# A two-block transformer in fp32r pieces: three buffers begin 9408 bytes later, and one product takes its matmuls in another order

## The chip, the cores and the metric

One core of a Trainium2 chip. The metric is the device time of one execution of the whole kernel in microseconds, the median of the runs.

## The reference

Two transformer-like blocks on one sequence of 256 tokens with 2048 features, all in float32. The first has causal differential attention and a gated linear recurrence side by side, attention to 256 memory rows, and a gated MLP with a causal convolution of three taps. The second has three convolution and pooling mixers and again such an MLP. Nearly all arithmetic is in 18 products with weight matrices. Those of the MLPs read

```
def conv_gated_mlp(h, w_up, conv_w, conv_b, w_down):
    up = h @ w_up                                      # 2048 -> 2 * 5632
    up = causal_depthwise_conv(up, conv_w) + conv_b
    gate, val = jnp.split(up, 2, axis=-1)
    return (jax.nn.silu(gate) * val) @ w_down          # 5632 -> 2048
```

## The kernel before

**Pieces of float32.** Each float32 operand is split in two fp32r pieces: a rounded part (hi) and its rest (lo). A product w x is computed as w_hi x_hi + w_hi x_lo + w_lo x_hi, summed in PSUM.

**Weights.** They come as 900 chunks of [128, 1024] (512 KB), one after another, through four slots. SyncE's queue loads a chunk into `raw`, ScalarE writes the rounded part into `w_hi` (line 784), VectorE the rest into `w_lo` (line 1325), TensorE multiplies and gives the slot back with the chunk's last matmul (`chunk_used`). A chunk holds 8 tiles of 128x128.

**Products, in the order of the run**, with their chunks: hg_fm 32, hg_i 16, da_fm 32, da_v 16, hg_g 16, mem_k 32, mem_v 32, out 32, mem_q 32, mem_o 32, up 176, down 88, conf 24, pool 8, gated 36, out_2 32, up_2 176, down_2 88. All plain matmuls go through the helper at line 2107. Four forms of order occur:

- Triples: for each tile w_hi with x_hi, w_hi with x_lo, w_lo with x_hi, 256 columns each, 24 matmuls in a chunk. Kind "F" and blocks without a kind in `product`: 148 chunks in hg_fm, mem_k, out, mem_q, mem_o, conf, pool and gated.
- Token-major in `product` (hg_i, da_v, mem_v: 64 chunks): the operand is stationary, the weights move, 512 columns, 12 matmuls in a chunk.
- Groups of four, two tiles in turn: a matmul of 512 columns takes the operand's hi and lo together with w_hi; it is done for two tiles, then w_lo with x_hi (256 columns) for the same two. 16 matmuls in a chunk. Kind "Q" in `product` (128 chunks in hg_fm, da_fm, hg_g, mem_k, out, mem_q, mem_o), and `TWO_TILES` in `product_halves` ("up" and up_2).
- Groups of four, `ROWS_TOGETHER` in `product_halves` ("down"): the same four matmuls, but for one tile and two rows k of the operand.

`product_tokens` (out_2, down_2) has tokens as output rows: per pair of slices hi with w_hi, hi with w_lo, lo with w_hi, 512 columns each, 12 in a chunk.

**The two orders of `product_halves`**, each a list of (kind, row, tile) for one chunk, are at lines 2209 and 2210. "up" and up_2 have 22 blocks of 8 chunks; a block fills four PSUM banks (one per tile), the next block the other four. VectorE and ScalarE read a block's banks once its last chunk is done; TensorE waits for that before it writes the same banks again two blocks later.

**Places.** `place` gives each buffer the next free bytes of the partition, from byte 16512 on. `raw`, `w_hi` and `w_lo` have 16384 bytes each; `x_res` (the residual x) has 16384 and `op` (the operand of most products, hi and lo of each of 16 slices side by side) 32768. Parameters, constants and small buffers follow with 9408 bytes together. Behind them begins the arena, at byte 124224, with everything else; `g` (the operand of "down" and down_2) and `y_hi` begin there. Some buffers are put on top of x and the operand by `x_at` and `op_at`.

Of the kernel before, what the change touches and what calls it, by code (L numbers as in the profile page):

```python
# [19 lines left out]
F32R = mybir.dt.float32r  # L20
# [5 lines left out]
P = 128  # L26
TOK = 256
DM = 2048
KT = DM // P
# [9 lines left out]
SLOTS = 4  # L39
CW = 1024  # L40
# [56 lines left out]
def plan():  # L97
    found, chunk, block = {}, 0, 0
    evac = {"act": 0, "dve": 0, "x": 0}
    for name, tiles, blocks, kt, token_major, reader in GEMMS:  # L100
        g = Gemm()
        g.name, g.tiles, g.blocks, g.kt, g.token_major, g.reader = name, tiles, blocks, kt, token_major, reader
        g.chunks = kt * tiles // 8
        g.first_chunk = chunk
        g.first_block = block
        g.banks = tiles // 2
        g.first_evac = evac[reader]
        g.before = found[GEMMS[len(found) - 1][0]] if found else None
        chunk += g.chunks * blocks
        block += blocks  # L110
        evac[reader] += g.banks * blocks
        g.end_chunk = chunk
        g.end_evac = evac[reader]
        found[name] = g
    return found, chunk
# [108 lines left out]
def build(nc, A):  # L224
    GM, NCHUNK = plan()
# [3 lines left out]
    with ctx:  # L229
        at = [16512]  # L230

        def place(name, shape, dt=F32, offset=None):
            size = 4
            for d in shape[1:]:
                size *= d
            where = at[0] if offset is None else offset
            if offset is None:
                at[0] += (size + 31) // 32 * 32
            return nc.alloc_sbuf_tensor_at(name, shape, dt, offset=where)
# [4 lines left out]

        raw = place("raw", [P, SLOTS, CW])
        w_hi = place("w_hi", [P, SLOTS, CW], F32R)
        w_lo = place("w_lo", [P, SLOTS, CW], F32R)
        x_at = at[0]
        x = place("x_res", [P, KT, TOK])
        op_at = at[0]  # L250
        op = place("op", [P, KT, 2, TOK], F32R)
        op_hi, op_lo = op[:, :, 0], op[:, :, 1]
        par = place("par", [P, NPAR])
        con = place("con", [P, NCON])
        small = place("small", [P, 64])
# [5 lines left out]
        tok_bias, tok_rstd = place("tok_bias", [P, 2]), place("tok_rstd", [P, 2])  # L261
        rstd = place("rstd", [P, 2, TOK])
        ones_r = place("ones_r", [P, P], F32R)
        arena = at[0]
        end = 229344
        room = end - arena
# [261 lines left out]
        def half_end(g, chunks):  # L528

            return [max(n for n, (of, _) in enumerate(chunks) if of == h) for h in range(4)]  # L530
# [784 lines left out]
        def _(dve):  # L1315
# [410 lines left out]
            def feed_forward(g, gd, turn, n, w, bname):  # L1726
# [6 lines left out]
                def gather(b, kind, parity):  # L1733
                    dve.wait_ge(first_kept, turn * g.blocks + 2 * b + kind + 1)
                    _, second = two_sums(parity, 0, 4)
                    TT(up[:, :, UPAD:UPAD + TOK], up[:, :, UPAD:UPAD + TOK], second, ALU.add).then_inc(dve_evac, 2)
# [368 lines left out]
        def _(pe):  # L2105
            def mm(out, lhsT, rhs, start, stop):
                return nc.tensor.matmul(out, lhsT, rhs, start=start, stop=stop, skip_group_check=True)  # L2107
# [101 lines left out]
            TWO_TILES = [(kind, r, 2 * u + t) for r in range(2) for u in range(2) for kind in (HI, LO) for t in range(2)]  # L2209
            ROWS_TOGETHER = [(kind, r, t) for t in range(4) for kind in (HI, LO) for r in range(2)]  # L2210

            def product_halves(g, both, ready, at=None, peeled=2, sequence=TWO_TILES):

                def one(b, parity):
                    static = isinstance(b, int)
                    if static:
                        past, pb_ = order[g.first_block + b - 2]
                        pe.wait_ge(evacs[past.reader], past.first_evac + past.banks * (pb_ + 1))  # L2220
                    else:
                        pe.wait_ge(evacs[g.reader], g.first_evac + g.banks * b - g.banks)
                    for c in range(g.chunks):
                        if at and static:
                            at(b, c)
                        s = (g.first_chunk + g.chunks * b + c) % SLOTS if static else c % SLOTS
                        pe.wait_ge(chunk_split, g.first_chunk + g.chunks * b + (c + 1))
                        if static and b == 0:
                            pe.wait_ge(operand_ready, ready(2 * c + 1))
                        for kind, row, t in sequence:  # L2230
                            k = 2 * c + row
                            cs = slice((4 * row + t) * P, (4 * row + t + 1) * P)
                            if kind == HI:
                                last = mm(ps[:, 4 * parity + t], w_hi[:, s, cs], both[:, k].rearrange("p a t -> p (a t)"), k == 0, False)
                            else:
                                last = mm(ps[:, 4 * parity + t, TOK:2 * TOK], w_lo[:, s, cs], both[:, k, 0], False, k == g.kt - 1)
                        last.then_inc(chunk_used, 1)

                for b in range(peeled):
                    one(b, (g.first_block + b) % 2)  # L2240
                pairs = (g.blocks - peeled) // 2
                if pairs:
                    with pe.Fori(0, pairs) as m:
                        for d in range(2):
                            one(2 * m + (peeled + d), (g.first_block + peeled + d) % 2)
# [28 lines left out]
            halves = lambda stage: (lambda k: READY[stage] + k // 2 + 1)  # L2274
# [264 lines left out]
            def beside_up(g, n):  # L2539

                def at(b, c):
                    if (b, c) == (1, 4):
                        pe.wait_ge(dve_evac, g.first_evac + g.banks)
                        sums(n)
                    if (b, c) == (2, 0):
                        pe.wait_ge(std_ready, STD_END[n])
                return at
# [86 lines left out]
            def turn_y(turn, j, t):  # L2634

                pe.wait_ge(y_scaled[t], 8 * turn + j + 1)
                for e in range(2):
                    f = 2 * j + e
                    bank = turn_banks(turn)[j]
                    last = nc.tensor.transpose(ps[:, bank, e * TOK + t * P:e * TOK + (t + 1) * P], y_tok[turn][:, t, f * P:(f + 1) * P], ident)  # L2640
                if t:
                    last.then_inc(y_turned, 1)
                elif j == 0:
                    last.then_inc(half_turned, 1)
# [32 lines left out]
            def beside_up_2():  # L2677
                sums_at = beside_up(GM["up_2"], 5)

                def at(b, c):  # L2680
                    if (b, c) == (0, 1):
                        turn_y(0, 2, 1)
                        turn_y(0, 3, 1)
                    for j in {1: (4, 5), 3: (6, 7)}.get(c, ()) if b == 0 else ():
                        pe.wait_ge(operand_ready, READY["up_2"] + j - 3)
                        turn_y(0, j, 0)
                        turn_y(0, j, 1)
                    sums_at(b, c)
                return at

            product_halves(GM["up_2"], op, halves("up_2"), beside_up_2(), 4, TWO_TILES)
            product_tokens(GM["down_2"], g_hi, g_lo, DOWN_2_CHUNKS, lambda pair: READY["down_2"] + 2 * pair + 2)
            for t in range(2):
                for q in range(4):
# [101 lines left out]
```

## Time and profile before

| | us |
|---|---|
| device time, median of 3 runs | 2654.44 |
| lowest, highest | 2654.02, 2654.53 |
| profiled execution: span, first to last instruction | 2652.2 |
| TensorE busy with matmuls | 2642.4 |
| VectorE busy | 1789.4 |
| ScalarE busy | 1345.5 |
| GpSimd busy | 150.3 |

The profiled execution has no device time of its own beside its span, so the span stands for it; the median of the runs is 2.2 us above it. Matmuls overlap: the next starts before the one before has ended, so their busy time says little, and the distance from start to start is what one costs. In the timeline, matmuls of one kind in a row are merged into one line with "x2", and the line's first number is the start of the first.

### The profile page before, as it was taken

How to read it: one execution, taken by the hardware profiler on the slowest of the kernel's cores; microseconds unless marked ns; L12 is line 12 of the kernel's file. 1: busy time of each engine (PE TensorE's matmuls, PEld its weight loads, DVE VectorE, ACT ScalarE, POOL GpSimd, SP SyncE). 2: the span in 40 equal slices, each digit the busy share in tenths (PEclk: the TensorE clock that was granted, in tenths of full speed). 3: DMA queues.
4: the chain of work that ended last, by engine and by line, in shares of the span. 5: the costliest groups of instructions: out<-in, count | busy, mean ns of one | idle time of the engine just before them, and what ended most of it. 6: DMA issues, size and time to landing. Idle time of an engine off the chain costs nothing.

```text
span 2652.2 us, 41690 instructions
## 1 busy us (share of the span) xinstructions
PE 2642.4 (100%) x15689; PEld 2332.9 (88%) x15689; DVE 1789.4 (67%) x2188; ACT 1345.5 (51%) x1647; POOL 150.3 (6%) x106
## 2 busy tenths in 40 slices
PE   9999999999999999999999999999999999999999
PEld 9888898889999888888888889998888888888887
DVE  7677567565645777777775456998777777776444
ACT  6554375464533655555553344444665555554443
POOL 2001200000200200000001222000020000000000
PEclk9999999999999999999999999999999999999999
DMA  8655456546545566566666665655566656656564
GB/s 260 192 160 187 139 182 185 178 154 203 177 129 167 184 192 189 188 188 188 188 189 191 190 190 173 196 187 174 168 191 190 190 189 187 187 188 206 191 192 148
DMA packets 256256, 487.12 MB, mean 184 GB/s; under 512 B 15069, under 2 KB 80629, under 8 KB 255616
## 3 DMA queue, kind: packets, MB, share of 16 engines
q1 hardware_dynamic: 254496, 476.11, 57.1%
q0 software_dynamic: 1488, 9.19, 1.0%
q8 instruction: 92, 1.51, 0.2%
q14 instruction: 36, 0.29, 0.0%
q10 hardware_dynamic: 144, 0.01, 0.0%
HBM read 483.12 MB, written 2.13 MB: 183 GB/s over the span
## 4 chain that ended last, share of the span: by engine, by line
PE 94%; DVE 4%; ACT 1%; POOL 1%; issue 0%; DVEq 0%; ACTq 0%; POOLq 0%
PE ps L2107 94%; DVE w_lo L1325 1%; DVE acc L1854 1%; POOL sumsq L724 1%; ACT w_hi L784 0%; DVE ya L1918 0%; DVE x_res L2088 0%; DVE ua L1359 0%; ACT lnz L1219 0%; PE ps L2640 0%; PE ps L2427 0%; DVE y_lo L1390 0%; DVE ya L1920 0%; DVE cvp L1908 0%; DVE ya L1914 0%
## 5 line engine op out<-in xcount | busy, mean ns | idle before, releaser
L1325 DVE TENSOR_TENSOR w_lo<-raw,w_hi 128x1024 fp32r<-128x1024 f32 x899 | 1119.2, 1247 | 785.6 <-ACT w_hi L784 784.4
L2107 PE MATMUL ps<-op,w_hi 128*128 128x512 f32 (+1 forms) x6208 | 1638.8, 353 | 0.1
L784 ACT ACTIVATE w_hi<-raw 128x1024 fp32r<-128x1024 f32 x899 | 949.4, 1059 | 1106.3 <-PE ps L2107 1088.2
L2107 PEld LDWEIGHTS ps<-op,w_lo 128*128 128x128 f32 x5024 | 948.4, 189 | 170.4
L2107 PE MATMUL ps<-op,w_lo 128*128 128x256 f32 x5024 | 1089.5, 279 | 0.0
L2107 PEld LDWEIGHTS ps<-op,w_hi 128*128 128x128 f32 x6208 | 955.2, 190 | 4.2 <-issue 1.8
L2107 PE MATMUL ps<-g,w_hi 128*128 128x512 f32 x704 | 219.6, 393 | 0.0
L2107 PE MATMUL ps<-w_hi,g 128*128 128x512 f32 x704 | 217.7, 390 | 0.0
L2107 PE MATMUL ps<-w_hi,op 128*128 128x512 f32 x512 | 163.5, 393 | 0.0
L2107 PEld LDWEIGHTS ps<-w_hi,g 128*128 128x128 f32 x704 | 132.1, 188 | 30.2
L2107 PEld LDWEIGHTS ps<-g,w_lo 128*128 128x128 f32 x704 | 132.4, 188 | 30.0
L2107 PE MATMUL ps<-g,w_lo 128*128 128x256 f32 x704 | 138.8, 279 | 0.0
L2107 PE MATMUL ps<-w_lo,g 128*128 128x512 f32 x352 | 138.7, 394 | 0.0
L2107 PEld LDWEIGHTS ps<-w_hi,op 128*128 128x128 f32 x512 | 96.1, 188 | 21.7 <-issue 1.3
L2107 PEld LDWEIGHTS ps<-g,w_hi 128*128 128x128 f32 x704 | 106.0, 188 | 0.0
L2107 PE MATMUL ps<-w_lo,op 128*128 128x512 f32 x256 | 99.8, 390 | 0.0
L2107 PEld LDWEIGHTS ps<-w_lo,g 128*128 128x128 f32 x352 | 66.2, 188 | 13.1
L1854 DVE SCALAR_TENSOR_TENSOR acc<-glu,par,acc 128x256 f32<-128x256 f32 x180 | 75.1, 478 | 0.0
L1751 DVE SCALAR_TENSOR_TENSOR cv<-up_s,par,cv 128x256 f32<-128x256 f32 x176 | 73.3, 478 | 0.0
L1751 DVE SCALAR_TENSOR_TENSOR cg<-up_s,par,cg 128x256 f32<-128x256 f32 x176 | 73.3, 478 | 0.0
L2107 PEld LDWEIGHTS ps<-w_lo,op 128*128 128x128 f32 x256 | 48.1, 188 | 9.3
L1740 DVE TENSOR_TENSOR up_s<-up_s,rstd 128x1024 f32<-128x1024 f32 x44 | 53.9, 1226 | 1.5
(318 smaller groups left out, 1534.6 us busy)
## 6 DMA issues: line engine op xcount, KB each, us to landing
raw<-in_weights SPq DMA_DIRECT2D x899, 512.0 KB, 4.5
x_res<-in_x SPq DMA_DIRECT2D x8, 256.0 KB, 5.6
mem_x<-in_mem POOLq DMA_DIRECT2D x1, 2048.0 KB, 8.8
x_res<-in_x POOLq DMA_DIRECT2D x1, 2048.0 KB, 9.9
w_row<-row_dram POOLq DMA_DIRECT2D x2, 1024.0 KB, 7.8
out_x<-x_res SPq DMA_DIRECT2D x3, 512.0 KB, 2.9
rel_rev<-rel_dram POOLq DMA_DIRECT2D x1, 1024.0 KB, 8.3
hg_con<-in_hg_consts POOLq DMA_DIRECT2D x1, 576.0 KB, 5.2
```

The costliest lines, as they stand in the source:

```text
L724: steps.inc(TT(sumsq[:, :, :], squares[:, 0] if j == 1 else sumsq[:, :, :], squares[:, j], ALU.add))
L784: nc.scalar.activation(w_hi[:, s], raw[:, s], ACT.Copy).then_inc(hi_rounded, 1)
L1325: TT(w_lo[:, s], raw[:, s], w_hi[:, s].bitcast(F32), ALU.subtract).then_inc(chunk_split, 1)
L1740: TT(up[:, :, UPAD:UPAD + TOK], up[:, :, UPAD:UPAD + TOK], spread(rstd[:, 1], 4), ALU.mult).then_inc(up_scaled, 1)
L1751: ins = STT(buf[:, t], up[:, t, tap:tap + TOK], col(tap, kind, t, b), buf[:, t], ALU.mult, ALU.add)
L1854: ins = STT(acc[:, i], glu[:, i, tap:tap + TOK], pc("conv_b_w_2", 6 * tap + i), acc[:, i], ALU.mult, ALU.add)
L2107: return nc.tensor.matmul(out, lhsT, rhs, start=start, stop=stop, skip_group_check=True)
```

## The change

The small buffers are placed ahead of `w_lo`, `x_res` and `op`, which so begin 9408 bytes later; the small buffers begin 65536 bytes earlier, and the arena stays where it was. In up_2 the order of a chunk's matmuls is `ROWS_TOGETHER` in place of `TWO_TILES`; "up" keeps `TWO_TILES`.

```diff
         raw = place("raw", [P, SLOTS, CW])
         w_hi = place("w_hi", [P, SLOTS, CW], F32R)
-        w_lo = place("w_lo", [P, SLOTS, CW], F32R)
-        x_at = at[0]
-        x = place("x_res", [P, KT, TOK])
-        op_at = at[0]
-        op = place("op", [P, KT, 2, TOK], F32R)
-        op_hi, op_lo = op[:, :, 0], op[:, :, 1]
         par = place("par", [P, NPAR])
         con = place("con", [P, NCON])
...
         rstd = place("rstd", [P, 2, TOK])
         ones_r = place("ones_r", [P, P], F32R)
+        w_lo = place("w_lo", [P, SLOTS, CW], F32R)
+        x_at = at[0]
+        x = place("x_res", [P, KT, TOK])
+        op_at = at[0]
+        op = place("op", [P, KT, 2, TOK], F32R)
+        op_hi, op_lo = op[:, :, 0], op[:, :, 1]
         arena = at[0]
...
-            product_halves(GM["up_2"], op, halves("up_2"), beside_up_2(), 4, TWO_TILES)
+            product_halves(GM["up_2"], op, halves("up_2"), beside_up_2(), 4, ROWS_TOGETHER)
```

The begin of a chunk of up_2 on TensorE, before the loop over its later blocks, the same in both kernels (`op` is the operand, `ps` the PSUM banks):

```order
L2107 MATMUL ps<-op,w_hi 128x512 [waits chunk_split]
L2107 MATMUL ps<-op,w_hi 128x512
L2107 MATMUL ps<-op,w_lo 128x256 x2
L2107 MATMUL ps<-op,w_hi 128x512 x2
L2107 MATMUL ps<-op,w_lo 128x256 x2
```

What moved isn't seen in such rows, since they name neither row nor tile. A group's first two matmuls were row 0 with tiles 0 and 1 and are now rows 0 and 1 with tile 0; the two with w_lo likewise. The first two wrote two banks and now write one.

## Rows read from the trace of the kernel before

**Rows 1.** The page: span, busy time and instructions by engine, granted clock, chain

```profile
span 2652.2 us, 41690 instructions
PE 2642.4 (100%) x15689; PEld 2332.9 (88%) x15689; DVE 1789.4 (67%) x2188; ACT 1345.5 (51%) x1647; POOL 150.3 (6%) x106
...
PEclk9999999999999999999999999999999999999999
...
PE 94%; DVE 4%; ACT 1%; POOL 1%; issue 0%; DVEq 0%; ACTq 0%; POOLq 0%
```

**Rows 2.** TensorE's waits, whole run: total us, times, longest us

```profile
PE ps L2107 <- DVE da_q L1412: 1.2, 1, 1.2
PE ps L2427 <- DVE attn L1654: 0.6, 1, 0.6
PE ps L2640 <- ACT y_tok L1244: 0.5, 1, 0.5
PE ps L2652 <- ACT y_tok L1244: 0.4, 1, 0.4
PE ps L2107 <- DVE w_lo L1325: 0.4, 2, 0.2
PE ps L2107 <- POOL sumsq L726: 0.4, 1, 0.4
```

**Rows 3.** The page's groups: busy us, mean ns, idle us before, releaser

```profile
L784 ACT ACTIVATE w_hi<-raw 128x1024 fp32r<-128x1024 f32 x899 | 949.4, 1059 | 1106.3 <-PE ps L2107 1088.2
```

**Rows 4.** TensorE in order of time, "up": start us, us, instruction

```profile
1000.02 0.63 PE L2107 MATMUL ps<-op,w_hi 128*128 128x512 f32 x2
...
1139.36 0.63 PE L2107 MATMUL ps<-op,w_hi 128*128 128x512 f32 x2
```

**Rows 5.** TensorE in order of time, up_2

```profile
2100.04 0.63 PE L2107 MATMUL ps<-op,w_hi 128*128 128x512 f32 x2
...
2239.37 0.63 PE L2107 MATMUL ps<-op,w_hi 128*128 128x512 f32 x2
```

**Rows 6.** TensorE in order of time, "down"

```profile
1400.45 0.39 PE L2107 MATMUL ps<-g,w_hi 128*128 128x512 f32 x1
...
1539.12 0.39 PE L2107 MATMUL ps<-g,w_hi 128*128 128x512 f32 x1
```

**Rows 7.** Busy us (x matmuls) by engine, clock, DMA share, GB/s: "up", up_2, "down"

```profile
1000.10:1139.30 139.20, 139.20 (x801) 121.44 (x800) 102.59 (x124) 75.82 (x86) 0.00 (x0) 1.00 0.60 188
2100.10:2239.35 139.25, 139.25 (x801) 121.48 (x801) 100.97 (x120) 77.53 (x90) 0.00 (x0) 1.00 0.61 188
1400.46:1539.10 138.64, 138.64 (x802) 121.62 (x801) 69.84 (x58) 53.03 (x51) 27.31 (x18) 1.00 0.62 190
```

**Rows 8.** TensorE in order of time, conf

```profile
1610.26 0.40 PE L2107 MATMUL ps<-op,w_hi 128*128 128x256 f32 x2
...
1610.62 0.40 PE L2107 MATMUL ps<-op,w_hi 128*128 128x256 f32 x2
```

**Rows 9.** TensorE in order of time, hg_i

```profile
129.95 0.84 PE L2107 MATMUL ps<-w_hi,op 128*128 128x512 f32 x3
...
131.31 0.84 PE L2107 MATMUL ps<-w_hi,op 128*128 128x512 f32 x3
```

**Rows 10.** TensorE in order of time, down_2

```profile
2499.64 0.62 PE L2107 MATMUL ps<-w_hi,g 128*128 128x512 f32 x2
...
2501.70 0.39 PE L2107 MATMUL ps<-w_hi,g 128*128 128x512 f32 x1
```

**Rows 11.** VectorE by line and shape, 900 to 1350 us ("up")

```profile
L1325 DVE TENSOR_TENSOR w_lo<-raw,w_hi 128x1024 fp32r<-128x1024 f32 x162 | 199.0, 1229 | 121.6 <-ACT w_hi L784 121.6
...
L1740 DVE TENSOR_TENSOR up_s<-up_s,rstd 128x1024 f32<-128x1024 f32 x20 | 24.5, 1226 | 0.7
```

## The prediction

> **What bounds the kernel now.** I read the page first, then who waited for whom on TensorE, then TensorE in order of time in one stage after another. [...] Busy time of pipelined matmuls proves little, so the waits have to confirm it: in the whole run TensorE's matmuls waited 3.5 us for anyone, in six lines [rows 2]. So the time is the sum of the distances from one matmul's start to the next one's. VectorE and ScalarE are ahead of it: most of ScalarE's idle time ends with TensorE giving back a slot of the weights [rows 3]. Only what changes TensorE's own pace, or makes another engine late by many microseconds, can be seen in the result.
>
> The pace is read from starts. A group of four matmuls (two of 512 columns with w_hi, two of 256 with w_lo) begins in "up" at 1000.02 us and, 200 groups later, at 1139.36: 139.34 / 200 = 696.7 ns [rows 4]. In up_2, which has the same order, it is 2239.37 - 2100.04 = 139.33, again 696.7 ns [rows 5]. In "down", which takes two rows of a tile together, it is 1539.12 - 1400.45 = 138.67, or 693.3 ns [rows 6]. (That 200 groups lie between is certain: one more or less would move the quotient by 3.5 ns per group, and the windows between count 800 or so matmuls with the one or two that lap over the edges [rows 7].) The granted clock is 1.00 in all three windows. The 3.3 ns are therefore no clock and no wait; something in the order or in the place of the operands costs them.
>
> What would be free of it? 1536 columns at 2.4 GHz take 640.0 ns, so "down" pays 53.3 ns above the columns, 13.3 per matmul. The products in triples pay the same: in conf three matmuls of 256 columns start every 0.36 us, 120 each, 13.3 above 106.7 [rows 8]; in hg_i six of 512 take 131.31 - 129.95 = 1.36 us, 226.7 each, 13.3 above 213.3 [rows 9]. So 13.3 ns is the floor that three different orders reach, and "up" and up_2 lie 3.3 ns per group above it. down_2 lies above it as well: nine matmuls in 2501.70 - 2499.64 = 2.06 us, 686.7 ns per three where hg_i has 680.0 [rows 10].
>
> **The change part by part.** Two edits; neither adds or removes an instruction, a transfer or a wait.
>
> *The order in up_2.* Its 22 blocks have 8 chunks each, 176 chunks of four groups. Each group keeps its four matmuls and their widths; only which row and tile they belong to changes. The nearest row is "down", with the same widths in the order that up_2 gets. At its pace a group saves 3.3 ns, a chunk 13.3 ns and the stage 176 x 13.3 = **2.35 us**, all of it on the path, since TensorE sets the pace there and nobody is made to wait longer: the weights' slot is given back by the last matmul of a chunk in either order, and the results are read only when a block's last chunk is done. But "down" differs from up_2 in a second thing, its moving operand g lies elsewhere. If the place and not the order gives "down" its pace, the edit gives nothing; and it could cost something, bounded by the largest excess that a row shows, 6.7 ns per three matmuls in down_2, taken once per group: 3.3 more than now, +2.35 us. I take the gain, because it is the row with the same widths and the same order, and keep -2.35 and +2.35 as ends.
>
> *The places.* From the shapes, w_hi begins at byte 32896, w_lo at 49280, the operand at 82048 and g at 124224. Modulo 128 these are 0, 0, 0 and 64. The shift of 9408 is 64 modulo 128, so w_lo and the operand move to 64, where g already is; w_hi stays. par, con and the other small buffers move down by exactly 65536 and keep all their low bits. Does the place cost anything? For VectorE the rows say no: a subtraction of 128x1024 with all its buffers at 0 takes 1229 ns in the middle of "up", a multiplication of up_s and rstd, both in the part that lies at 64, takes 1226 [rows 11]; I put nothing on VectorE, ScalarE and the transfers, and ScalarE's idle 1106.3 of 2652.2 us, nearly all behind TensorE, would cover some per cent more [rows 3]. For TensorE the large distances seem free: each window of 50 chunks goes twelve times round the four slots and six times through the operand's 16 rows, and two such windows agree to 0.01 us [rows 4, 5]. Only the low bits are open, since within one stage they never change. They could be worth anything from the best to the worst of the rivals below, -4.0 to +9.6 us over the other stages. I take 0, as the floor of 13.3 is reached both with moving operand and weights at 0 (hg_i, conf) and with g at 64 against weights at 0 ("down").
>
> *What is late next.* At the start of up_2 TensorE does wait, for 0.4 to 0.5 us at a time, for ScalarE and VectorE to hand over the turned rows [rows 2]. A chunk that is 13 ns shorter makes these waits 13 ns longer, so the first two or three chunks gain nothing: under 0.05 us, left out.
>
> Sum: the profiled span of 2652.2 becomes 2649.85. The times shown are device times, 2654.44 in the median (2654.02 to 2654.53), 2.2 us above the span, which I take to stay: **2652.1 us**, 0.09% less. A measurement of this kernel can tell about 0.2%, 5.3 us, from no change, so the forecast is "within 0.2%".
>
> **The rivals.**
>
> *Places at 64 give the pace of "down" to every two-tile order (faster).* Speaks for it: "down" is the only stage of such groups whose moving operand lies at 64, and the only one at the floor. Against: conf and hg_i reach the floor at 0. Besides up_2 the two-tile order runs in 176 chunks of "up" and in 128 chunks of the earlier products. Then 304 x 13.3 = 4.05 us more are saved: 2648.0 us, 0.24% less.
>
> *Operands 64 bytes apart cost the triples 6.7 ns (slower).* Speaks for it: the two kinds of triples in the trace differ just so. hg_i and conf have both operands at 0 and the floor [rows 8, 9]; down_2 has weights and moving operand 64 apart and 6.7 ns more per three [rows 10]. After the change w_hi is 64 away from the operand in all products of conf's and hg_i's form. These are 148 chunks of eight triples, 148 x 8 x 6.7 = 7.9 us, and 64 chunks of four, 1.7 us. Against: "down" is 64 apart too and at the floor, and the order of tokens in down_2 differs from hg_i's. Price: 2652.1 + 9.6 = 2661.7 us. It decides from 7.7 us of excess (2.35 + 5.3), four fifths of the full price or 5.3 ns on each of the 1,440 triples; below that the result is not slower by more than 0.2%.
>
> *The order does nothing in up_2.* Then the 3.3 ns belong to this operand, or to writing over two banks in turn with these widths, and nothing else moves: 2654.4 us. The two windows differ in order and place at once [rows 5, 6], so the trace can't exclude it. [...]
>
> **How the numbers follow.** The forecast 0.48; the order without effect 0.17; faster by places 0.20; slower by places 0.15. The first two stay within 0.2%, so faster 0.20, same 0.65, slower 0.15. The forecast's own bounds are 2652.1 to 2656.8 (the +2.35 end). The range also reaches below to the places' gain, 2648.0, with 1 us for the measurement, and above half-way into the places' cost: 2647.0 to 2658.0. What is left out is mostly the full price of the slower rival, 0.15.
>
> **What would show it.** Right: in up_2 200 groups take 138.67 us, in "up" still 139.34, in "down" 138.67, in conf 0.36 us per triple, nine matmuls of down_2 still 2.06 us. If 200 groups of "up" take 138.67 as well, the place counts, and the faster rival stands. If conf's triples take over 0.36 or hg_i's six over 1.36 us, the slower one. If up_2 keeps 139.33 while all the rest stands still, the order has no part in it. I would be wrong in kind if TensorE's waits grew beyond 3.5 us, which nothing here explains, or if VectorE's 1229 ns rose past 1250, since then a place would count for VectorE.

## The result and the profile after

The changed kernel takes 2694.74 us in the median of five runs (2693.78 to 2695.54), the kernel before 2654.28 in the same rounds: the ratio is 1.0153, with a 95% interval of 1.0142 to 1.0164. It is slower by 40.5 us, where I had forecast 2.3 us less. The page's lines that answer to [rows 1]:

```profile
span 2692.4 us, 41690 instructions
PE 2682.4 (100%) x15689; PEld 2348.6 (87%) x15689; DVE 1793.3 (67%) x2188; ACT 1345.5 (50%) x1647; POOL 150.9 (6%) x106
...
PEclk9999999999999999999999999999999999999999
...
PE 96%; DVE 3%; ACT 0%; issue 0%; DVEq 0%; ACTq 0%
```

The span grew by 40.2 us and TensorE's busy time by 40.0, at the same mean granted clock (0.999 in both profiled executions) and the same number of matmuls. It is not a wait. TensorE's matmuls wait for others 3.7 us in all, 3.5 before [rows 2]:

```profile
PE ps L2107 <- DVE da_q L1412: 1.2, 1, 1.2
PE ps L2107 <- DVE w_lo L1325: 1.0, 1, 1.0
PE ps L2427 <- DVE attn L1654: 0.6, 1, 0.6
PE ps L2640 <- ACT y_tok L1244: 0.5, 1, 0.5
PE ps L2652 <- ACT y_tok L1244: 0.4, 1, 0.4
```

TensorE itself is slower from one matmul to the next. In order of time (start us, us, instruction), 200 groups of four in "up", then in "down", then in up_2:

```profile
1000.41 0.63 PE L2107 MATMUL ps<-op,w_hi 128*128 128x512 f32 x2
...
1143.07 0.64 PE L2107 MATMUL ps<-op,w_hi 128*128 128x512 f32 x2
...
1400.59 0.63 PE L2107 MATMUL ps<-g,w_hi 128*128 128x512 f32 x2
...
1543.25 0.64 PE L2107 MATMUL ps<-g,w_hi 128*128 128x512 f32 x2
...
2100.64 0.64 PE L2107 MATMUL ps<-op,w_hi 128*128 128x512 f32 x2
...
2243.30 0.63 PE L2107 MATMUL ps<-op,w_hi 128*128 128x512 f32 x2
```

"up" takes 142.66 us for its 200 groups, 713.3 ns each, where [rows 4] gave 696.7. "down", whose code and whose operand the change does not touch, takes 142.66 as well (693.3 before [rows 6]). up_2, in its new order, takes 142.66 too (696.7 before [rows 5]). Both orders run at one pace now, and it is worse than either was.

The other forms, one window from each of hg_i, conf and down_2:

```profile
130.49 0.87 PE L2107 MATMUL ps<-w_hi,op 128*128 128x512 f32 x3
...
131.88 0.86 PE L2107 MATMUL ps<-w_hi,op 128*128 128x512 f32 x3
...
1636.68 0.40 PE L2107 MATMUL ps<-op,w_hi 128*128 128x256 f32 x2
...
1640.21 0.40 PE L2107 MATMUL ps<-op,w_hi 128*128 128x256 f32 x2
...
2500.06 0.63 PE L2107 MATMUL ps<-w_hi,g 128*128 128x512 f32 x2
...
2502.16 0.63 PE L2107 MATMUL ps<-w_hi,g 128*128 128x512 f32 x2
```

Six matmuls of hg_i take 1.39 us (1.36 before [rows 9]). In conf ten triples lie between the two rows: 3.53 us, 353 ns each, where a triple took 360 [rows 8]. So the triples became *faster*, below what I had called the floor. Nine matmuls of down_2 take 2.10 us (2.06 before [rows 10]).

The loss adds up from the paces. Chunks of groups of four got 66.7 ns longer in 480 cases (4 x 16.7) and 80 ns in "down"'s 88; hg_i's form (12 matmuls) 66.7 ns in 64 chunks, down_2's 53.3 ns in 120; the triples 53.3 ns shorter in 148. That is 32.0 + 7.0 + 4.3 + 6.4 - 7.9 = 41.8 us, against 40.2 in the spans.

VectorE, in the same window as [rows 11], shows no loss:

```profile
L1325 DVE TENSOR_TENSOR w_lo<-raw,w_hi 128x1024 fp32r<-128x1024 f32 x159 | 196.9, 1238 | 128.7 <-ACT w_hi L784 127.8
...
L1740 DVE TENSOR_TENSOR up_s<-up_s,rstd 128x1024 f32<-128x1024 f32 x20 | 24.5, 1225 | 0.7
```

### The profile page after: what moved, and what is told of

It is laid out like the page before. It is cut to its first block, busy times and chain, and to the rows that moved or that the text cites. A ratio compares the mean times of both kernels' runs of the same rounds, so it can differ in the third digit from the quotient of the medians.

```text
span 2692.4 us, 41690 instructions
## 1 busy us (share of the span) xinstructions
PE 2682.4 (100%) x15689; PEld 2348.6 (87%) x15689; DVE 1793.3 (67%) x2188; ACT 1345.5 (50%) x1647; POOL 150.9 (6%) x106
## 3 DMA queue, kind: packets, MB, share of 16 engines
q1 hardware_dynamic: 254496, 476.11, 53.3%
## 4 chain that ended last, share of the span: by engine, by line
PE 96%; DVE 3%; ACT 0%; issue 0%; DVEq 0%; ACTq 0%
PE ps L2107 96%; DVE acc L1854 1%; DVE w_lo L1325 1%; DVE ya L1918 0%; DVE x_res L2088 0%; DVE ua L1359 0%; PE ps L2640 0%; PE ps L2427 0%; DVE y_lo L1390 0%; DVE ya L1920 0%; ACT w_hi L784 0%; DVE cvp L1908 0%; DVE ya L1914 0%; PE ps L2495 0%; DVE rstd L1382 0%
## 5 line engine op out<-in xcount | busy, mean ns | idle before, releaser
L2107 PE MATMUL ps<-op,w_lo 128*128 128x256 f32 x5024 | 1112.9, 283 | 0.0
L2107 PEld LDWEIGHTS ps<-w_lo,g 128*128 128x128 f32 x352 | 66.3, 188 | 15.6
```

## The experiments

Distances are given as (operand, w_lo): how many bytes past their old places the moving operand and w_lo begin, modulo 256, with w_hi fixed. Before the change the products that read `op` are at (0, 0). "down" and down_2 read g, which is 192 bytes past such a place, so they are at (192, 0). The change makes it (192, 192) for all of them.

The expectations name several theories by letters. Theory D, given in full with the map below, is: TensorE's pace depends on the distance between moving and stationary operand, modulo a small power of two, and on nothing else. A buffer that a diff places earlier has lost its old line further down; those removed lines are left out.

**The places alone, and the order alone.** The first kernel has the change's places and up_2's old order, the second the old places and

```diff
-            product_halves(GM["up_2"], op, halves("up_2"), beside_up_2(), 4, TWO_TILES)
+            product_halves(GM["up_2"], op, halves("up_2"), beside_up_2(), 4, ROWS_TOGETHER)
```

> Edit: the new places, with up_2 left in its old order (two tiles in turn). In the changed kernel all stages of groups of four ran at 713.3 ns per group, in either order. Theory P (places make the whole loss, the order none of it): up_2 at 713.3 ns per group as well, time 2694.7 us within 0.5. Rival O (the new order at the new places has a part in the loss): up_2 faster than 713.3 ns, time below 2694.

> Edit: the old places, with up_2 in the new order. If order counts at the old places, as I forecast: up_2 at 693.3 ns per group in place of 696.7, 2.35 us less, 2651.9 us. If the place of g gave down its pace: up_2 at 696.7 or slower, 2654.3 us or up to 2656.6.

Measured: places alone 2695.1 us, ratio 1.0154 (1.0139 to 1.017). Order alone 2653.68 against 2653.89, ratio 0.9999 (0.999 to 1.0009). TensorE in up_2 with the places alone:

```profile
2100.00 0.63 PE L2107 MATMUL ps<-op,w_hi 128*128 128x512 f32 x2
...
2242.67 0.64 PE L2107 MATMUL ps<-op,w_hi 128*128 128x512 f32 x2
```

142.67 us for 200 groups, the same as the changed kernel with the other order. TensorE in up_2 with the order alone:

```profile
2100.21 0.63 PE L2107 MATMUL ps<-op,w_hi 128*128 128x512 f32 x2
...
2239.54 0.63 PE L2107 MATMUL ps<-op,w_hi 128*128 128x512 f32 x2
```

139.33 us, to 0.01 us what the old order took [rows 5]. The order does nothing at either place. The 40 us are the places'. So were the 3.3 ns between "up" and "down" that I had given to the order, as the kernel with the operand alone moved shows below.

**How far.** Two shifts in the old order, 64 bytes (only tok_bias and tok_rstd ahead of w_lo) and 9344 (all small buffers but these).

```diff
+        tok_bias, tok_rstd = place("tok_bias", [P, 2]), place("tok_rstd", [P, 2])
         w_lo = place("w_lo", [P, SLOTS, CW], F32R)
...
-        tok_bias, tok_rstd = place("tok_bias", [P, 2]), place("tok_rstd", [P, 2])
```

> Edit: old order, only 64 bytes (tok_bias, tok_rstd) placed ahead of w_lo, so w_lo, x and the operand begin 64 bytes later in place of 9408. Theory L (the lowest 7 bits of the addresses decide, 9408 is 64 modulo 128): the same paces as in the changed kernel, 713.3 ns per group, 117.8 ns per matmul of the triples, 2694.7 us. Rival H (a distance of hundreds or thousands of bytes decides): the old paces, 2654.3 us.

> Edit: old order, a shift of 9344 bytes, which is 0 modulo 128 and has nearly all of the distance. Theory L (lowest 7 bits): the old paces, 696.7 ns per group in up and up_2, 693.3 in down, 2654.3 us. Rival H (the distance): the changed kernel's, 713.3 ns and 2694.7 us.

Both theories fell. A shift of 64 gives 2659.71 us, ratio 1.0022 (1.0012 to 1.0031); one of 9344, which is 0 modulo 128, gives 2671.52, ratio 1.0067 (1.0051 to 1.0082). 200 groups of "up", shifted by 64:

```profile
1000.45 0.62 PE L2107 MATMUL ps<-op,w_hi 128*128 128x512 f32 x2
...
1140.45 0.63 PE L2107 MATMUL ps<-op,w_hi 128*128 128x512 f32 x2
```

And shifted by 9344, "up", then "down":

```profile
1000.30 0.64 PE L2107 MATMUL ps<-op,w_hi 128*128 128x512 f32 x2
...
1141.64 0.64 PE L2107 MATMUL ps<-op,w_hi 128*128 128x512 f32 x2
...
1400.51 0.62 PE L2107 MATMUL ps<-g,w_hi 128*128 128x512 f32 x2
...
1539.18 0.62 PE L2107 MATMUL ps<-g,w_hi 128*128 128x512 f32 x2
```

140.00 us, 700.0 ns per group at 64. At 9344 it is 141.34, 706.7 ns, in "up" and 138.67, the old 693.3, in "down". With 713.3 at 9408 the groups of "up" rise as 696.7, 700.0, 706.7, 713.3: 9344 is 128 and 9408 is 192 modulo 256. That suggested a period. One detail fits no single pace per distance: shifted by 64, "up" runs at 700.0 ns per group and up_2, in the same order and at the same places, at 698.3.

**The period.** The shift as 192 bytes (w_pair and the two small ones ahead of w_lo) and as 256 (the buffer `small`).

> Edit: old order, shift of w_lo, x and the operand by 192 bytes. 9408 is 192 modulo 256, 512 and 1024. Theory D with a period of at most 1024: every stage at the changed kernel's pace, 713.3 ns per group of four, 2694.7 us. Rival (bits from 1024 up count too): a time between 2654 and 2694 with other paces.

> Edit: old order, shift by 256 bytes. Theory D with period 256: the old paces everywhere, 2653.9 us. With period 512 or more: other paces, in the direction of the changed kernel's, above 2660 us.

The diffs are below. Measured: 192 bytes 2694.95 us, ratio 1.0154 (1.0138 to 1.0171), and 142.66 us per 200 groups of "up"; 256 bytes 2653.95, ratio 1.0 (0.999 to 1.0009), and 139.34 us. The shift of 9408 acts as one of 192, and one of 256 as none.

```diff
+        w_pair = place("w_pair", [P, 2, KT])
+        tok_bias, tok_rstd = place("tok_bias", [P, 2]), place("tok_rstd", [P, 2])
         w_lo = place("w_lo", [P, SLOTS, CW], F32R)
```

```diff
+        small = place("small", [P, 64])
         w_lo = place("w_lo", [P, SLOTS, CW], F32R)
```

**One buffer at a time.** In the first kernel x and the operand begin 9408 bytes later and w_lo stays; in the second w_lo begins 192 bytes later and the operand 256.

```diff
         w_lo = place("w_lo", [P, SLOTS, CW], F32R)
+        par = place("par", [P, NPAR])
...
+        ones_r = place("ones_r", [P, P], F32R)
         x_at = at[0]
```

```diff
+        w_pair = place("w_pair", [P, 2, KT])
+        tok_bias, tok_rstd = place("tok_bias", [P, 2]), place("tok_rstd", [P, 2])
         w_lo = place("w_lo", [P, SLOTS, CW], F32R)
+        relb = place("relb", [P, HEADS])
+        tok_sums = place("tok_sums", [P, 2, 4])
         x_at = at[0]
```

> Edit: old order; w_lo stays at its old place, x and the operand begin 9408 bytes later. Then the operand is 192 bytes (modulo 256) from both w_hi and w_lo, as g was in down before the change. Theory D: up and up_2 at the pace that down had, 693.3 ns per group of four in spite of the other order; down unchanged at 693.3, down_2 at 686.7 per three; hg_i at down_2's 686.7; the triples between 117.8 and 120 ns. Time 2641 to 2650 us, faster than before. Rival W (the operand's own place costs): up at 713.3 ns, time about 2680 us.

> Edit: old order; only w_lo moved, by 192 bytes as by 9408 modulo 256; x and the operand by 256, which counts as 0. The map gives for (operand 0, w_lo 192): up and up_2 693.2 ns per group, triples 354.2, hg_i's form 690.8, down 713.2, down_2's form 700.0. Sum: 3.1 us more, 2656.9 us. So neither part of the shift alone should cost much (operand alone: 2633.7), and the 40 us should need both. Rival (w_lo's place by itself is what costs): 2680 us or more.

The operand alone: 2633.74 us, ratio 0.9924 (0.9908 to 0.9941), *faster* than before by 20 us. TensorE in "up", then in conf:

```profile
1000.67 0.62 PE L2107 MATMUL ps<-op,w_hi 128*128 128x512 f32 x2
...
1139.34 0.62 PE L2107 MATMUL ps<-op,w_hi 128*128 128x512 f32 x2
...
1635.75 0.39 PE L2107 MATMUL ps<-op,w_hi 128*128 128x256 f32 x2
...
1639.15 0.39 PE L2107 MATMUL ps<-op,w_hi 128*128 128x256 f32 x2
```

"up" runs at 138.67 us per 200 groups, the pace of "down" before [rows 6], in its old order. Ten triples of conf take 3.40 us, 340 ns each (360 before). I had allowed the triples 353 ns at best; at 340 they can save 148 x 8 x 13.3 = 15.8 us more, and in the stages that reach 340 they do, which explains a result 7 us under the lower bound that I had set. w_lo alone: 2657.62 us, ratio 1.0016 (1.0007 to 1.0026), with "up" at 693.3 and the loss in "down", which now is at (192, 192):

```profile
1400.71 0.63 PE L2107 MATMUL ps<-g,w_hi 128*128 128x512 f32 x2
...
1543.37 0.64 PE L2107 MATMUL ps<-g,w_hi 128*128 128x512 f32 x2
```

142.66 us again. So neither move by itself makes the loss: one gains 20 us, the other costs 3.9. What costs 713.3 ns is the pair (192, 192), whichever product is at it.

**A map.** A kernel in which TensorE runs alone, with 324 short streams, each run once: 256 of the kernel's four forms at all pairs of distances in steps of 32 bytes, and 68 of 512-column matmuls of one pair of buffers in steps of 64. Its w_hi begins at a multiple of 256, the whole kernel's 128 bytes beyond one.

```
w_hi at 32768, w_lo at 40960, op at 49152; a, b: offsets of op and w_lo
group of four, eight times:
    mm(ps[:, t], w_hi[:, tile], op[:, a:a + 512])              for t in 0, 1
    mm(ps[:, t, 256:512], w_lo[:, tile + b], op[:, a:a + 256])  for t in 0, 1
```

> No part of the reference is computed: after x is loaded and rounded, TensorE alone runs short streams of matmuls of the kernel's four forms, with the operand placed 0 to 224 bytes and w_lo 0 to 224 bytes beyond multiples of 256, and one stream of 512-column matmuls with the operand 0 to 4032 bytes on. VectorE, ScalarE and the transfers are idle meanwhile. Theory D (TensorE's pace depends on the distance between moving and stationary operand, modulo a small power of two, and on nothing else): the streams give the paces of the kernel at the same distances: group of four 696.7 ns at (0, 0), 713.3 at (192 to w_hi, 0 to w_lo), 693.3 at (192, 192), triples 120 ns per matmul at (0, 0) and 117.8 at (192, 0), and the long scan repeats with its period. Rival C (contention: the pace needs VectorE's and ScalarE's traffic on the same buffers): all streams at the floor, one pace for all distances.

For the groups and triples the pairs in this expectation are the operand's distances to w_hi and to w_lo. What it calls (192, 0) is (192, 192) in the notation of this text, and its (192, 192) is (192, 0).

Two streams of groups of four in it, at (0, 0) and at (192, 192), three groups between the first two rows and three between the last two:

```profile
20.95 0.63 PE L54 MATMUL ps<-op,w_hi 128*128 128x512 f32 x2
...
23.04 0.63 PE L54 MATMUL ps<-op,w_hi 128*128 128x512 f32 x2
...
329.44 0.64 PE L54 MATMUL ps<-op,w_hi 128*128 128x512 f32 x2
...
331.58 0.64 PE L54 MATMUL ps<-op,w_hi 128*128 128x512 f32 x2
```

2.09 us against 2.14, 697 and 713 ns. The rival fell: VectorE, ScalarE and the transfers are idle here (from 20 to 1556 us TensorE has 8050 matmuls, VectorE and ScalarE no instruction, and the DMA share is 0.00), and the paces are there all the same. Theory D got the paces that it named, but its "on nothing else" did not hold, as the exceptions below show. The table has the second halves of the streams, when the pace has settled, beside the stages of the whole kernels at the same distances (ns per group of four, or per three matmuls):

| form | distance | map | stage, kernel |
|---|---|---|---|
| group of four | (0, 0) | 696.5 | 696.7, "up" before |
| | (192, 0) | 693.2 | 693.3, "down" before |
| | (64, 64) | 700.0 | 700.0, "up", shift 64 |
| | (128, 128) | 706.8 | 706.7, "up", shift 9344 |
| | (192, 192) | 713.2 | 713.3, all, changed kernel |
| triple of 256 | (0, 0) | 360.0 | 360, conf before |
| | (192, 192) | 353.2 | 353, conf, changed kernel |
| | (192, 0) | 353.2 | 340, conf, operand alone |
| | (192, 128) | 340.0 | 340, conf, three places |
| hg_i's form | (0, 0) | 680.0 | 680.0, before |
| | (192, 192) | 696.5 | 696.7, changed kernel |
| down_2's form | (192, 0) | 686.8 | 686.7, before |
| | (192, 192) | 700.0 | 700.0, changed kernel |

All rows of the table but one agree within 0.5 ns, although w_hi lies at different places modulo 256 in the two kernels; so the distances count here and not the absolute places. The table does not hold every case. With w_lo alone moved, hg_i's form ran at 695.5 ns per three where the map has 690.8, and the triples at 353.3 where it has 354.2. The row that disagrees has two settled paces, 353.2 in the map and 340 in conf; in the kernel with the operand alone, `gated` changes from the one to the other after the mixer's matmuls come between two chunks (its first block runs at 340 ns per triple, its last at 353). What set the pace of conf apart from the map was not tried. The long scan repeats every 256 bytes over 4032: 512-column matmuls of one pair of buffers start every 226.6 to 228.1 ns at 0, 229.2 at 64, 232.1 at 128 and 233.2 at 192. In four further streams the weights begin 64 bytes on and the columns 64, 128, 192 and 256: distances of 0, 64, 128 and 192 again. They start every 226.6, 228.5, 233.4 and 233.3 ns, near the paces of the same distances in the scan but up to 1.3 ns off.

Weighted with the kernel's chunks, the map's paces give a sum for each kernel, beside what was measured (us against before):

| kernel | distance | map's sum | measured |
|---|---|---|---|
| shift 64 | (64, 64) | +7.9 | +5.8 |
| shift 9344 | (128, 128) | +18.5 | +17.6 |
| changed kernel | (192, 192) | +41.8 | +40.5 |
| w_lo alone | (0, 192) | +3.1 | +3.9 |
| operand alone | (192, 0) | -12.5 | -20.0 |
| three places (next experiment) | (192, 128) | -24.2 | -18.8 |

The operand alone gains more than its sum because its triples reach 340 ns in most stages.

**The best place of the map.** Weighted with the kernel's chunks, the lowest sum is at (192, 128): `decay` (128 bytes) ahead of w_lo, tok_bias and tok_rstd (64) between w_lo and x.

```diff
+        decay = place("decay", [P, HEADS, NCHK])
         w_lo = place("w_lo", [P, SLOTS, CW], F32R)
+        tok_bias, tok_rstd = place("tok_bias", [P, 2]), place("tok_rstd", [P, 2])
         x_at = at[0]
```

> Edit: old order; w_lo begins 128 bytes later, x and the operand 192 bytes later, the arena stays. The map of paces by distances gives for (operand 192, w_lo 128): groups of four 693.5 ns, triples 340.0 (from 360.0), hg_i's form 693.5 (from 680.0), down 693.5, down_2's form 690.2 (from 686.7). Summed over the chunks: 24.2 us less, 2629.6 us. Rival (the sum over chunks doesn't hold, since steady paces need some matmuls to settle after every wait): less than half of it, above 2641.

2634.85 us, ratio 0.993 (0.9917 to 0.9944), 18.8 us less than before. That is 5 us less gain than the map's sum, and more than half of it, so the rival's 2641 was not reached either. The paces came as the map has them: ten triples of conf in 3.40 us,

```profile
1639.79 0.39 PE L2107 MATMUL ps<-op,w_hi 128*128 128x256 f32 x2
...
1643.19 0.39 PE L2107 MATMUL ps<-op,w_hi 128*128 128x256 f32 x2
```

and "up" 693.3 per group. But faster triples met another limit. out_2 grew from 94.20 to 98.43 us, since VectorE is late with the weights' rests there. The row that had 0.4 us in [rows 2] has become

```profile
PE ps L2107 <- DVE w_lo L1325: 3.7, 2, 2.8
```

In the trace VectorE has no gap by then: before the wait it does four steps of the convolution of 31 taps (line 1854) between one rest and the next, and it is busy nearly all the time. So it is before the change (59.93 of the 60 us from 1750 to 1810), where TensorE's longer chunks leave it enough. Busy us of VectorE, with the operand and w_lo at the three places, before and around the waits (x instructions, clock, DMA share, GB/s):

```profile
1745.00:1760.00 15.00, 15.00 (x27) 1.00 0.57 204
1790.00:1805.00 15.00, 14.93 (x29) 1.00 0.44 141
```

No kernel with that work moved elsewhere was run. Matmuls of down_2's form at (192, 128) are slower too (243.17 us for down_2, 241.61 before), but that is in the map's sum and explains none of the 5 us. The kernel with the operand alone stays as good: the two medians, 2633.74 and 2634.85, come from different rounds and differ by less than can be told apart.

**Widths and types.** TensorE alone again, streams of 24 matmuls.

```
mm(ps[:, t, 0:n], w_hi[:, t * P:(t + 1) * P], op[:, a // 4:a // 4 + n])      # fp32r
mm(ps[:, t, 0:n], w_b[:, t * P:(t + 1) * P], op_b[:, a // 2:a // 2 + n])     # bf16
```

> No part of the reference is computed: TensorE alone runs streams of 24 matmuls at distances of 0 to 256 bytes in steps of 32, in fp32r with 128, 256, 384 and 512 columns and in bf16 with 128, 256 and 512, and in fp32r with one stationary tile throughout. Theory D' (the loss comes from loading 4-byte weights beside a 4-byte moving stream): fp32r streams show 226.6 to 233 ns at 512 columns as in the scan before, by distance, and bf16 shows no dependence on the distance and less above its columns than 13 ns. Rival (the loss belongs to any pair of addresses): bf16 depends on the distance too, by several ns.

A stream of 24 bf16 matmuls 96 bytes off, and 23 matmuls each of two fp32r streams with one stationary tile, at 0 and at 96 bytes (start us, us from the first start to the last end):

```profile
236.55 5.36 PE L59 MATMUL ps<-op_b,w_b 128*128 128x512 bf16 x24
...
294.74 5.40 PE L59 MATMUL ps<-op,w_hi 128*128 128x512 f32 x23
...
311.65 5.53 PE L59 MATMUL ps<-op,w_hi 128*128 128x512 f32 x23
```

In bf16 every distance gives 55.8 ns at 128 columns, 109.2 at 256 and 215.8 at 512. In fp32r 256 columns take 113.3 ns (64 bytes off) to 120.0 (0, 96 and 256 off), 384 take 173.3 to 176.7, and 512 take 226.7 (0) to 234.3 (160); with one stationary tile throughout it is the same, and its weights are still loaded again and again (2026 loads beside 2021 matmuls in the whole kernel). So in these streams fp32r has the dependence and bf16 has none. The theory's reason, the load of 4-byte weights, was not tested by itself: the two types may differ in more than the size of an element.

The slope from width to width is the same in both types: in bf16 (215.8 - 55.8) / 384, in fp32r at distance 0 (226.7 - 120.0) / 256, both 0.417 ns per column, which is 2.4 columns per ns.

The fp32r streams with 128 columns can't be used. Their matmuls start every 213.3 ns at every distance, but they ran first, up to 66 us, and the run was slow until 70 us. The stream of 256 columns that follows shows it: within it the starts are 213.3 ns apart up to 70 us, which is 1.2 columns per ns, and 116 to 121 ns apart after that, without a wait between. Here are the matmuls of 256 columns in the window 66.3 to 69.6 us, 16 of them, and in the shorter window 70.8 to 73.5 us, 25 (busy us, mean ns, idle us):

```profile
L59 PE MATMUL ps<-op,w_hi 128*128 128x256 f32 x16 | 3.7, 420 | 0.0
...
L59 PE MATMUL ps<-op,w_hi 128*128 128x256 f32 x25 | 3.2, 283 | 0.0
```

The next kernel begins alike: its first matmuls of 512 columns start every 427 ns up to 22.3 us, and every 226.7 ns after that. The profile's clock column reads 1.00 before and after the change of pace in both kernels, so here the spacing has to be read beside it; what ends the slow stretch, no run shows. The 120.0 at distance 0 is from the stream with one stationary tile, which begins at 267.9 us.

**Whose weights?** One more, on whether the distance to the matmul's own weights counts or that to the next one's, which are loaded meanwhile: from 20 to 290 us of its trace matmuls run for 270.0 us and weight loads for 236.3, 1551 of each, and the load for the next matmul starts about 5 ns after a matmul does.

```
w = u % 2 * d                       # where the weights of matmul u begin
m = {"same": d, "own": w, "next": d - w}[kind]   # where its columns begin; "same" has w = 0
mm(ps[:, u % 4, 0:n], w_hi[:, w:w + P], op[:, m:m + n])
```

> No part of the reference is computed: TensorE alone runs streams of 32 fp32r matmuls of 512 and of 256 columns. Weights begin at 0 and at d in turn (modulo 256). In the streams 'own' the moving columns begin where the same matmul's weights do, in the streams 'next' where the next matmul's weights do; in the streams 'same' the weights stay at 0 and the columns at d. Theory N (what costs is the load of the next matmul's weights, which runs beside the columns of this one): 'next' keeps the pace of distance 0, 226.7 ns at 512 columns, for every d, while 'own' lies at 229 to 234 ns as 'same' does. Rival (the distance to the matmul's own weights counts): the reverse, 'own' at 226.7 for every d and 'next' at 229 to 234.

Neither. At 512 columns and d = 64, "same" takes 229.1, "own" 231.6, "next" 233.3 ns; at d = 128 they take 233.3, 228.4 and 230.0. At 256 columns "next" takes 116.5 to 120.4 for d other than 0. Neither kind kept the pace of distance 0 for every d, so neither the distance to a matmul's own weights nor that to the next one's sets the pace alone. Which rule does, these runs don't give.

## Why the prediction was wrong, point by point

- *What bounds the kernel* held: TensorE's pace, at a mean granted clock of 0.999 before and after, with waits of 3.5 and 3.7 us. The consequence was in the text ("only what changes TensorE's own pace ... can be seen") but not drawn to its end: with 15,689 matmuls in a row, 1 ns on each is 15.7 us. A term priced at 0 there needed a range in ns per matmul.
- *The order in up_2*, -2.35 us: wrong. Measured 139.33 us per 200 groups in either order at the old places, 142.67 and 142.66 at the new. I had two windows that differed in order and in place and gave the difference to the order. The rival "the order does nothing" was right in that half, at 0.17.
- *The places*, "I take 0": this is the step that failed: a term put at 0 that measured 41 us (2695.1 against 2653.89 with the places alone). It rested on "the floor of 13.3 is reached both with ... 0 and with g at 64 against weights at 0". There is no such floor: conf ran at 117.8 ns per matmul in the changed kernel and at 113.3 with three places, 6.7 above its columns. (The 2.4 GHz behind the columns' share are what two rows give: 256 columns more cost 226.7 - 120.0 = 106.7 ns [rows 8, 9], 2.4 columns per ns.) That three forms met at 13.3 ns was a coincidence of three entries of the map.
- *Modulo 128*: wrong, the paces repeat with 256, and w_lo counts beside w_hi. At 128 the new "up" seemed to be a place that "down" already showed. In fact the pair (192, 192) occurred nowhere in the kernel before, so no row could price it. "Down" was at (192, 0), and I had noticed neither that w_lo's move changes "down" too nor that w_hi and w_lo would now differ. The bounds of -4.0 and +9.6 came from pairs that did occur.
- *The faster rival* had a true core, at the wrong kernel: with the operand alone moved, every two-tile stage takes the pace of "down" (the expectation for the operand alone drew on it), and 20 us are gained. With w_lo moved along it is lost.
- *The slower rival* had the right kind (operands apart by a small distance) and the wrong part: it laid the cost on the triples, which got faster by 2.2 ns per matmul, and not on the groups of four, which carry 39.0 of the 41.8 us. Of its terms hg_i's form did get slower, by 4.3 us where it had 1.7; the 6.4 us of down_2's form it left out.
- *VectorE, ScalarE, transfers at nothing*: held. VectorE's subtraction took 1238 ns against 1229, under the 1250 I had named, and nobody waited for it much longer.
- *The large distances are free*: held, with 256 and 9408 against 192 as the proof.

## What to carry to other kernels

Where TensorE runs fp32r matmuls back to back, the starting addresses of stationary and moving operands are a tuning knob that was worth from 0.8% faster to 1.5% slower here, and any edit that shifts a buffer can turn it without meaning to. Read the start-to-start distance per stage and form, compare with what the columns alone cost (0.417 ns each here, from the slope between two widths), and note each operand's address modulo 256 beside it. Two stages that differ in order and in address can't tell which of the two makes a difference; a kernel of short streams that scans the addresses can. Most of its entries carried over to the full kernel within 0.5 ns, but a stream with two settled paces was 13 ns off, so the choice still has to be run in the full kernel.

## What the runs showed of the hardware

- In these kernels and streams, how often fp32r matmuls start depends on where the operands lie to each other modulo 256 bytes: 512 columns every 226.7 to 234.3 ns, 256 columns every 113.3 to 120.0, with as many weight loads as matmuls (8069 of each in the map). From 20 to 1556 us of the map VectorE, ScalarE and GpSimd have no instruction and the DMA share is 0.00, so there it isn't contention with other engines.
- The bf16 streams have none of it: 55.8, 109.2 and 215.8 ns for 128, 256 and 512 columns at every distance, which is 0.417 ns per column and 2.5 ns above the columns. In fp32r 512 columns take 11 to 18.5 ns more than in bf16.
- In the first 70 us of the kernel of widths fp32r matmuls start every 213.3 ns, with 128 columns as well as with 256, at a clock column of 1.00. What 128 fp32r columns take after that no run here shows.
- The settled pace can have two values for one stream (340 or 353 ns per triple at (192, 0); 113.3 or 117.8 ns per matmul at 192 in two runs of single-pair streams). In `gated` it changed after other matmuls came between; what sets it in general is open. Why the paces repeat with 256, and what rule joins the two operands' places, stays open too.
